# The last layer norm of a hybrid decoder layer: be2 stored ahead, the result added by the transfer, rstd applied by ScalarE

## The reference, cut to what matters

```python
def _layer_norm(x, g, b):
    xf = x.astype(jnp.float32)
    mu = xf.mean(-1, keepdims=True)
    var = jnp.square(xf - mu).mean(-1, keepdims=True)
    return ((xf - mu) * lax.rsqrt(var + LN_EPS) * g + b).astype(x.dtype)

# per layer (DEPTH = 1)
        x = _layer_norm(ALPHA * x + gate1 * (y @ w_out[l]), ln1_g[l], ln1_b[l])
        u = x * (1.0 + scale2) + shift2
        f = _grouped_moe(u, router_w, router_b, moe_w_gate[l], moe_w_up[l], moe_w_down[l])
        x = _layer_norm(ALPHA * x + gate2 * f, ln2_g[l], ln2_b[l])
```

## Time and profile before

| | |
|---|---|
| three executions | 753.3, 754.45, 755.13 us; median 754.45 |
| the profiled execution | 755.41 us |
| its span, first to last instruction | 753.3 us |
| mean granted TensorE clock | 0.946 of full speed |
| PE, DVE, ACT, POOL busy, of the span | 87%, 47%, 30%, 13% |
| from POOL's first gather of the tail to the end of the span | 723.4 to 753.3 us |
| DVE's last instruction ends | 750.23 us |

### The profile page before, as it was taken

The page is one execution under the profiler, slowest core; times in us unless marked ns, Lnnn a source line. Parts: engine busy times, 40 slices in busy tenths (PEclk is TensorE's granted clock), DMA queues, the critical chain, the costliest instruction groups (busy, mean ns, idle before and its releaser), DMA issues.

```text
span 753.3 us, 15566 instructions
## 1 busy us (share of the span) xinstructions
PE 652.9 (87%) x6011; PEld 430.4 (57%) x6012; DVE 352.4 (47%) x691; ACT 226.9 (30%) x471; POOL 98.7 (13%) x185
## 2 busy tenths in 40 slices
PE   0799999998989799999999659799999999999910
PEld 0276666676767577777788445355555555555500
DVE  0265444378888786666756673211111111111117
ACT  0233533557554454555600401001111111111112
POOL 0131001110000000000000012122222222222240
PEclk9999999999999899999999858899999999999965
DMA  9999766293211222223692899999999999991156
GB/s 300 374 323 308 260 224 228 90 329 101 85 57 56 85 85 82 59 61 104 218 422 118 328 411 358 418 419 416 421 418 418 418 419 418 417 372 42 42 141 215
DMA packets 83924, 189.41 MB, mean 251 GB/s; under 512 B 7432, under 2 KB 60008, under 8 KB 68528
## 3 DMA queue, kind: packets, MB, share of 16 engines
q1 hardware_dynamic: 67664, 148.66, 52.3%
q0 software_dynamic: 7376, 32.26, 12.5%
q10 hardware_dynamic: 8848, 8.01, 3.2%
HBM read 174.83 MB, written 14.07 MB: 251 GB/s over the span
## 4 chain that ended last, share of the span: by engine, by line
PE 67%; DVE 11%; DMA 9%; ACT 5%; issue 5%; SPq 2%; POOL 1%; ACTq 0%; POOLq 0%; DVEq 0%
PE psum L1488 20%; PE psum L1499 10%; DMA raw<-in_w_in_dram 7%; PE psum L1290 7%; PE psum L1292 6%; PE psum L1291 6%; PE psum L1478 2%; PE psum L1471 2%; PE psum L1411 2%; PE psum L1413 2%; PE psum L1412 2%; PE psum L1256 2%; SPq L396 1%; PE psum L1333 1%; ACT ssb L731 1%
## 5 line engine op out<-in xcount | busy, mean ns | idle before, releaser
L1488 PE MATMUL psum<-wg,xs 128*32 128x256 f32 x1280 | 150.7, 390 | 0.5 <-ACT xs L791 0.5
L1488 PE MATMUL psum<-wu,xs 128*32 128x256 f32 x1280 | 150.8, 390 | 0.0
L1290 PE MATMUL psum<-uh,whi 128*128 128x512 f32 x336 | 138.3, 412 | 0.1
L1291 PE MATMUL psum<-ul,whi 128*128 128x512 f32 x336 | 132.0, 393 | 0.0
L1292 PE MATMUL psum<-uh,wlo 128*128 128x512 f32 x336 | 132.0, 393 | 0.0
L1488 PEld LDWEIGHTS psum<-wg,xs 128*32 128x32 f32 x1280 | 72.6, 112 | 53.9 <-issue 5.2
L785 ACT ACTIVATE hsil<-psum 64x256 f32<-64x256 f32 x40 | 15.0, 376 | 230.9 <-PE psum L1488 230.9
L864 DVE TENSOR_TENSOR wlo<-raw,whi 128x1024 fp32r<-128x1024 f32 x42 | 51.4, 1224 | 68.4 <-ACT whi L615 68.3
L1171 DVE TENSOR_TENSOR h_sb<-psum,hsil 64x256 f32<-64x256 f32 x40 | 17.1, 428 | 139.4 <-ACT hsil L785 139.4
L1499 PE MATMUL psum<-wd,hT 128*32 128x256 f32 x1280 | 77.4, 382 | 1.1 <-DVE hT L1177 1.1
L1290 PEld LDWEIGHTS psum<-uh,whi 128*128 128x128 f32 x336 | 63.8, 190 | 21.1 <-issue 7.6
(11 more groups left out here) (252 smaller groups left out, 832.6 us busy)
## 6 DMA issues: line engine op xcount, KB each, us to landing
wg<-in_moe_w_gate_dram SPq DMA_DIRECT2D x32, 1024.0 KB
wu<-in_moe_w_up_dram SPq DMA_DIRECT2D x32, 1024.0 KB
wd<-in_moe_w_down_dram SPq DMA_DIRECT2D x32, 1024.0 KB
raw<-in_w_in_dram SPq DMA_DIRECT2D x42, 512.0 KB, 3.9
ada<-in_ada_w_dram POOLq DMA_DIRECT2D x16, 1024.0 KB, 7.0
ada<-in_ada_w_dram SPq DMA_DIRECT2D x8, 1024.0 KB, 17.0
y_d<-ysb ACTq DMA_DIRECT2D x160, 32.0 KB
y_d<-zrow POOLq DMA_DIRECT2D x8, 512.0 KB, 6.5
```

Source lines behind the costliest of these rows:

```text
L1290: mmul(bank[s % 2], h[:, k, :], uh[:, k, :], start=(k == 0), stop=False)
L1291: mmul(bank[s % 2], h[:, k, :], ul[:, k, :], start=False, stop=False)
L1488: ins = mmul(psum[32 * g:32 * g + 32, 0, 0:256], xs[:, k % 2, k // 2, :], wgu[slot][g // 2][:, k, (g % 2) * 256:(g % 2) * 256 + 256], star ...
```

## The change

The shift be2 is stored to all four tiles of `out` by SP, behind the last weights. DVE makes only (z - mean) * g2, now into `fin[t][1]`, as soon as minus the mean is there, and then the reciprocal of the root. ACT multiplies by rstd, from `fin[t][1]` into `fin[t][0]`. POOL stores that with a transfer that adds to what `out` holds, after it has waited for the stores of be2. The square's unused result goes to `fin[t][2]`. The first gather of tile 1 becomes a plain one into `fin[1][1]`, and DVE adds it, as it does for tile 0. POOL waits for the four adding stores at its end.

```diff
@@ SP
             refill(15, 0, last)
+            sp.wait_ge(rows_in, 16 * 5)
             for t in range(NT):
-                sp.wait_ge(S["fin_out"], t + 1)
-                sp.dma_start(out[0, t * P:(t + 1) * P, :], fin[t][0][:, :]).then_inc(out_st, 16)
+                sp.dma_start(out[0, t * P:(t + 1) * P, :], be2r[:, :]).then_inc(out_base, 16)
+            sp.wait_ge(out_base, 16 * NT)
             sp.wait_ge(out_st, 16 * NT)
@@ POOL
-                if t == 0:
+                if t <= 1:
                     pool.indirect_dma_start(fin[t][1][:, :], None, y_d, at_row[0]).then_inc(fgather[t], 16)
                 else:
                     pool.indirect_dma_start(x1[:, t, :], None, y_d, at_row[0], compute_op=ALU.add).then_inc(fgather[t], 16)
                 pool.indirect_dma_start(fin[t][2][:, :], None, y_d, at_row[1]).then_inc(fgather[t], 16)
 
+            pool.wait_ge(out_base, 16 * NT)
+            for t in range(NT):
+                pool.wait_ge(S["fin_out"], t + 1)
+                pool.dma_start(out[0, t * P:(t + 1) * P, :], fin[t][0][:, :], accum_op=ALU.add).then_inc(out_st, 16)
+            pool.wait_ge(out_st, 16 * NT)
@@ ACT
             def moments(t):
-                z, spare = fin[t][0][:, :], fin[t][1][:, :]
+                z, spare = fin[t][0][:, :], fin[t][2][:, :]
...
+            def scaled(t):
+                act.wait_ge(S["fin_g"], t + 1)
+                act.wait_ge(S["fin_r"], t + 1)
+                A(fin[t][0][:, :], fin[t][1][:, :], ACT.Copy, scale=rstd[:, t:t + 1]).then_inc(S["fin_out"], 1)
+
             for t in range(NT):
                 moments(t)
+                if t >= 1:
+                    scaled(t - 1)
+            scaled(NT - 1)
@@ DVE
                 dve.wait_ge(fgather[t], 32)
-                if t == 0:
+                if t <= 1:
                     chain(V.tensor_tensor(x1[:, t, :], x1[:, t, :], ya_[:, :], ALU.add))
...
             def normalise(t):
                 z, ya_, yb_ = fin[t]
+                dve.wait_ge(S["fin_s"], 2 * t + 1)
+                V.scalar_tensor_tensor(ya_[:, :], z[:, :], fsum[:, t, 1:2], g2r[:, :], ALU.add, ALU.mult)\
+                    .then_inc(S["fin_g"], 1)
                 dve.wait_ge(S["fin_sqrt"], t + 1)
-                chain(V.reciprocal(rstd[:, t:t + 1], rstd[:, t:t + 1]))
-                chain(V.scalar_tensor_tensor(z[:, :], z[:, :], fsum[:, t, 1:2], g2r[:, :], ALU.add, ALU.mult))
-                V.scalar_tensor_tensor(z[:, :], z[:, :], rstd[:, t:t + 1], be2r[:, :], ALU.mult, ALU.add)\
-                    .then_inc(S["fin_out"], 1)
+                V.reciprocal(rstd[:, t:t + 1], rstd[:, t:t + 1]).then_inc(S["fin_r"], 1)
```

More of the change, by code:

```diff
@@ L357, in hybrid_layer @@
         y_st = [sem(f"y_st{i}") for i in range(4)]
-        out_st = sem("out_st")
+        out_st, out_base = sem("out_st"), sem("out_base")
         fgather = [sem(f"fgather{i}") for i in range(NT)]
@@ L366, in hybrid_layer @@
             rt_exp_in rt_exp m_done pos_ps ctrl_done pool_went pe_went y_zero z_done idx_ready onehots idx_ps slotw wcol_ps
-            fin_z fin_s fin_sqrt xT_m_ps xgs_rdy xs_rdy gu_ps silu_done h_done_m
+            fin_z fin_s fin_g fin_r fin_sqrt xT_m_ps xgs_rdy xs_rdy gu_ps silu_done h_done_m
             hT_ps hT_sb d_ps y_ev fin_n fin_out v_ps v_sb idn_done pool_in t_done""".split()
```

## The result

The changed kernel takes 765.82 us (median of 4, 764.37 to 766.47) against 754.79 us for the kernel before on the same chip (median of 4). The ratio is 1.014, 95% interval 1.0117 to 1.0162: slower by some 11 us. The forecast was 754.6 with a range to 757.3.

What follows compares the result with a forecast made beforehand. The tail after POOL's first gather was taken to be bound by DVE's work, the gathers just under it. 2.4 us gained against 2.5 lost on stores gave +0.15 us on the 754.45 median: 754.6, range 752.4 to 757.3.

Steps and rivals of the forecast that it cites:

- Where the gain comes from: DVE and ACT after tile 3's landing: the last result is ready at 747.8 instead of 750.2, 2.4 us earlier.
- The price of an adding gather: POOL's gathers in the tail: a plain one moves in 1.9 us, which leaves 1.9 to 3.7 us for an adding one.
- be2 ahead at nothing: SP's four be2 stores behind the last weights: 5 us of movement in an empty DMA stretch, taken as 0.
- tile 1's gather near nothing: Tile 1 gathered plainly: lands 0.7 us earlier, but DVE's added 1.22 us leaves tile 1 no gain; only later tiles land earlier.
- The adding stores, 2.0 us of movement: POOL's final stores: each adding store moves for 2.0 us, between 1.3 for a plain store and 3.7.
- rival 2: POOL's four adding stores queue up, each waiting for the one before if it moves over about 2.9 us; 757.7, chance 0.15.
- 5.25 us where it cost 2.7: Store path from last result to last landing: 5.25 us instead of 2.7, 2.5 us lost against the 2.4 gained.
- With 0.4 behind it the span ends: End of the kernel: the last store lands at 753.05 and the span ends 0.4 us later, at 753.45.

## Why the prediction was wrong

**Where the gain comes from: right.** "The last result is ready at 747.8 instead of 750.2": it was 746.1, of which 0.8 us are an earlier start (POOL's first gather at 722.6 instead of 723.4). Counted from that first gather the result was ready 23.1 to 23.5 us later in six profiles with the new split, against 25.8 to 26.8 in four without it: some 3 us, where I had 2.4. ACT's multiplication took 1.13 us (I had 1.15), the last reciprocal ended 3.76 us after tile 3's sum began (I had 4.15), and that sum did wait for a gather. Tile 3 landed 18.3 us after POOL's first gather began, where I had 19.0 and it was 19.9 before; a plain gather in place of an adding one saves more than I took:

**The price of an adding gather: wrong.** I took 1.9 us off each pair for a plain gather, from the rate of 727 to 729, and so had 1.9 for the adding one "near the lower end". A plain packet of 4 KB takes 0.16 us, so 8 per engine are 1.3 us; 3.8 - 1.3 = 2.5 us was left for the adding one, and the packets of the changed kernel confirm it (0.33 us in the record of one, 0.38 with the stalls between). The stretch from 727 to 729 held more than plain packets: of its 134 packets of 4 KB, 101 took 0.16 us and 27 took 0.3 us and more. Its rate gave a plain gather too dear and, by subtraction, an adding one too cheap.

**be2 ahead at nothing, and tile 1's gather near nothing: right**, each run alone, to within the 2 us of their intervals.

**The adding stores, 2.0 us of movement: this step failed in its size.** They moved in 3.2, and then they queue. That is rival 2 and its formula: gathers landed at 740.9, and 740.9 + 4 x 3.2 + 0.5 = 754.2, against 755.3 measured. The sum fits better than the steps: the four landed at 745.9, 748.4, 750.8 and 755.3, so the third, 5.5 us after its issue, took little longer than one alone (5.2), and the last stretch of 4.5 us has the thin end shown above. I gave rival 2 0.15, with the argument that POOL issues nothing more by then; but after POOL's last issue had ended, at 747.2, the packets took 0.38 us all the same. The price "5.25 us where it cost 2.7", from the last result to its landing, is near right where only the last store adds (5.5), and was 9.2. The term is +6.6 us instead of +2.5.

The Trainium skill's fit for such a transfer, from "DMA: Bandwidth & Descriptors", "Anatomy of one DMA — SWDGE (gpsimd) path" (3.2 us for this size), agrees with the plain stores of POOL, 2.9 to 3.5 us. It does not hold for adding ones (5.2 to 8.9 us).

**"With 0.4 behind it the span ends": this step failed.** I carried the 0.4 us of the kernel before over to a program in which POOL, not SP, issues last and waits last. What stood there was 8.5 us, with POOL's drain of 8.07: a term of 8.1 us put at nothing, twice the 4.1 us that the stores were off. Without it the time would have come out at the upper end of the range (757.3): 765.8 - 8.1 = 757.7, or 756.9 by the landing at 755.3 in my own sum. None of my rivals had it. The row was in the trace: POOL's program ended at 747.2, 11.8 us behind its last busy instruction, and my sum was made of busy instructions and transfers alone. By that row, the last issue of my own sum, which ended at 749.35, would have put the drain's end near 761, 8 us behind the span that I forecast.

## What to carry to other kernels

When an edit moves the last transfer to another engine, price the end of that engine's program too. Sequencer rows at the closing line are part of the tail: a drain that is hidden now is exposed once that engine issues later, or waits at its end. Here whatever GpSimd issues as a DMA should have landed some 4 us, and been issued some 8 us, before the program's other engines are done, and GpSimd should wait for nothing at its end that another engine can wait for. An adding store frees a vector instruction of 1.3 us and costs 2.1 us of latency alone, and twice the DMA time of a plain one in a queue: at the last tile it costs more than it frees, and for earlier tiles no gain was measured (0.999, 0.9974 to 1.0006).

## What the hardware showed that was not expected

- GpSimd's closing DRAIN takes 7.7 to 8.1 us after an end wait, even when its own last transfer landed 10 us before; SP's takes 7 ns. The Trainium skill, in "VectorE: DVE Perf Modes", "The DRAIN you can't avoid", tells of DRAINs of about 12 ns on all five engines, from the code that stands around every kernel. The closing rows of SP and PE are as short here (7 and 8 ns); those of ACT and DVE take 0.3 to 1.3 us, but begin beside their engine's last instruction and end some 0.05 us after it; GpSimd's is the one that adds time. What it does in its 8 us stays open.
- Without the end wait it ends 3.9 to 4.1 us after the last landing (seven profiles) or, where that is earlier, 8.1 us after the last issue (one profile).
- A 4 KB packet of an adding transfer takes 328 ns at a DMA engine (median), a plain one 159 ns, whether it adds in SBUF or in HBM.
- The wait view put SP's 8.2 us down to PE, which had long been done. At the closing line the name in that view can't be relied on; the ends of the drains tell which engine was last.
